# A decoder step on one core: the sample tile of the token-major projection on four column tiles, the late convolution taps over seven tiles, and the convolution's state stored in the next stage

## The reference

```python
def mix_inputs(x, pos, ln1, w_in):
    p = rmsnorm(x, ln1) @ w_in
    conv_in = p[..., :CONV_CH] * jax.nn.sigmoid(p[..., CONV_CH:2 * CONV_CH])
    # the other 1304 columns: q (512), three K/V pairs (768), gates (24)
    q = apply_rope(q, pos); keys of the three K/V pairs rotated too
    gates = jax.nn.sigmoid(p[..., o:o + COL_GATE])

def conv_module(a_ext, dw_w, dw_b, ln_g, ln_b):
    y = depthwise_conv(a_ext, dw_w, width 31) + dw_b
    return silu(layernorm(y, ln_g, ln_b))
...
p_conv.append(a[:, t_p - (CONV_W - 1):])      # out8: last 30 GLU rows of the prompt
s_conv.append(a_ext[:, a.shape[1]:])          # out9: the convolution's state of the 8 samples
```

## Time and profile before

| | |
|---|---|
| median of 3 runs | 1791.72 us (1790.69 to 1794.85) |
| time of the profiled execution | 1789.7 us |
| its span, first to last instruction | 1788.1 us |
| busy, share of the span | PE 80%, PEld 47%, DVE 37%, ACT 21%, POOL 11% |
| first stage | 0 to 339.2 us |
| second stage | 339.2 to 463.6 us |
| token-major projection of tile 8 | 305.2 to 322.8 us |

### The profile page before, as it was taken

One profiled execution on the slowest core, in us unless ns is written; L12 is line 12 of the kernel. 1 busy time (PEld: TensorE's weight loads), 2 busy tenths in 40 slices (PEclk: granted clock), 3 DMA queues, 4 the chain that ended last, 5 costly groups with the idle time before them and its releaser, 6 DMA issues. The chain is left out here.

```text
span 1788.1 us, 22662 instructions
## 1 busy us (share of the span) xinstructions
PE 1432.3 (80%) x7436; PEld 833.6 (47%) x7436; DVE 666.8 (37%) x1324; ACT 371.9 (21%) x794; POOL 192.7 (11%) x348
## 2 busy tenths in 40 slices
PE   6999899467679888852489971799999999999960
PEld 4665444267545555532245531344544454444430
DVE  2596676601258666636312237010110011011007
ACT  4000100220236555441111110111111111111113
POOL 0000011262100000003100000011111111111111
PEclk9999999779659999986689985799999999999985
DMA  6500000374331000024521100999999999999927
GB/s 240 223 1 6 12 21 21 143 218 140 89 99 32 1 1 1 1 65 123 169 101 59 63 17 31 385 412 415 398 411 411 401 409 410 409 390 409 408 104 289
DMA packets 82876, 336.98 MB, mean 188 GB/s; under 512 B 9818, under 2 KB 45787, under 8 KB 64818
## 3 DMA queue, kind: packets, MB, share of 16 engines
q1 hardware_dynamic: 64986, 287.76, 41.4%
q0 software_dynamic: 15440, 47.30, 7.7%
q10 hardware_dynamic: 2384, 1.06, 0.2%
HBM read 311.20 MB, written 29.45 MB: 191 GB/s over the span
## 5 line engine op out<-in xcount | busy, mean ns | idle before, releaser
L1695 PE MATMUL ps<-arena 128*128 128x512 f32 x544 | 241.1, 600 | 0.0
L1695 PEld LDWEIGHTS ps<-arena 128*128 128x128 f32 x544 | 102.5, 191 | 137.7 <-issue 137.6
L346 PE MATMUL ps<-arena 128*128 128x512 f32 (+3 forms) x432 | 158.9, 527 | 0.0
L499 DVE SCALAR_TENSOR_TENSOR arena<-arena 128x1024 f32<-128x1024 f32 x120 | 147.7, 1283 | 1.3
L1396 PE MATMUL ps<-arena 128*128 128x512 f32 (+1 forms) x288 | 129.6, 603 | 15.3 <-DVE arena L1491 15.3
L1749 PE MATMUL ps<-arena 128*128 128x512 f32 x272 | 120.1, 593 | 6.3 <-DMA arena<-scratch_h,ints 6.3
L1703 PE MATMUL ps<-arena 128*64 128x256 f32 x1088 | 121.2, 380 | 0.0
L301 PE MATMUL ps<-arena 128*128 128x352 f32 x384 | 116.2, 464 | 4.2 <-issue 3.7
L1000 ACT ACTIVATE arena<-ps,arena 128x640 f32<-128x640 f32 (+7 forms) x128 | 90.0, 703 | 118.6 <-DVE arena L1075 104.7
L346 PEld LDWEIGHTS ps<-arena 128*128 128x128 f32 (+1 forms) x432 | 77.2, 180 | 79.3 <-issue 72.0
L913 PE MATMUL ps<-arena 128*128 128x128 f32 x528 | 82.2, 286 | 35.8 <-ACT arena L1010 32.1
(11 more groups left out here) (357 smaller groups left out, 1588.1 us busy)
## 6 DMA issues: line engine op xcount, KB each, us to landing
arena<-in_w_gate SPq DMA_DIRECT2D x34, 2048.0 KB, 11.3
arena<-in_w_up SPq DMA_DIRECT2D x34, 2048.0 KB, 15.9
arena<-in_w_down SPq DMA_DIRECT2D x34, 2048.0 KB, 16.1
arena<-in_x_prompt SPq DMA_DIRECT2D x16, 512.0 KB, 6.7
arena<-in_cache_cmp POOLq DMA_DIRECT2D x64, 128.0 KB, 3.3
arena<-in_cache_cmp SPq DMA_DIRECT2D x64, 128.0 KB, 2.9
arena<-in_cache_sel SPq DMA_DIRECT2D x64, 128.0 KB, 2.2
arena<-scratch_y SPq DMA_DIRECT2D x16, 512.0 KB, 5.9
```

The costliest lines, as they stand in the source:

```text
L346: mm = pe.matmul(ps[:n, b + o // 512, 0:w], xT[:, k, t * P:t * P + n], w_tm[:, k, o:o + w], start=(k == 0), stop=(k == KT_ - 1))
L499: ins = dve.scalar_tensor_tensor(o, i, dw[:, c, j:j + 1], o, ALU.mult, ALU.add)
L1695: mm = pe.matmul(ps[:, bank, :], xgT_l[:, k, :], w[LARGE][:, k, :], start=(k == 0), stop=(k == KT_ - 1))
```

## The change

It has three parts. **Tile 8 of the projection** no longer runs in three pieces over the full array. Its 1304 columns are cut into four of 326 (`QTR`), and each `k` step issues four matmuls, one on each column tile of the array (32 columns wide, at 0, 32, 64 and 96), with the same stationary tokens and a quarter of the columns each. The four results lie in one PSUM bank, on the four groups of 32 partitions, and ACT brings them together by four copies (326, 326, 326 and 302 columns) and the sigmoid. **The late taps** are shared over seven tiles: `share` is 9, so tiles 0 to 5 have nine, tile 6 has eight, and tiles 7 and 8 none. **The convolution's state** is copied by ACT into `state_p` and `state_s`, in that part of `A4` which `w_cmp1` does not reach; this place lies over `a_p`, so ACT waits until all taps have been done. The five DMAs are issued by POOL in the second stage, between its loads of round 1 and the additions; POOL waits for them at that stage's end.

```diff
+        state_p, state_s = flat(A4 + 3536, CH), flat(A4 + 3536 + CH, CH)
+        QTR = COLS_TM // 4
@@ PE, projection of tile t
-                    for o, w in ((0, 512), (512, 512), (1024, COLS_TM - 1024)):
+                    if t < NQ:
+                        for o, w in ((0, 512), (512, 512), (1024, COLS_TM - 1024)):
+                            for k in range(KT_):
+                                mm = pe.matmul(ps[:n, b + o // 512, 0:w], xT[:, k, t * P:t * P + n],
+                                               w_tm[:, k, o:o + w], start=(k == 0), stop=(k == KT_ - 1))
+                    else:
                         for k in range(KT_):
-                            mm = pe.matmul(ps[:n, b + o // 512, 0:w], xT[:, k, t * P:t * P + n],
-                                           w_tm[:, k, o:o + w], start=(k == 0), stop=(k == KT_ - 1))
+                            for q in range(4):
+                                mm = pe.matmul(ps[n * q:n * q + n, b, 0:QTR], xT[:, k, t * P:t * P + n],
+                                               w_tm[:, k, QTR * q:QTR * q + QTR], start=(k == 0),
+                                               stop=(k == KT_ - 1), tile_position=(0, n * q))
@@ ACT, copies of tile t
+                    else:
+                        for q in range(4):
+                            m = min(QTR, 1280 - QTR * q)
+                            act.activation(p_sb[:n, t % 2, QTR * q:QTR * q + m], ps[n * q:n * q + n, b, 0:m], ACT.Copy)
+                        logit = ps[3 * n:4 * n, b, QTR - 24:QTR]
+                    act.activation(gates[:n, t, :], logit, ACT.Sigmoid).then_inc(sem("tm_copied"), 1)
@@ ACT, end of the first stage
-                act.wait_ge(sem("qk_turned"), TILES)
-                act.activation(xin[:TAPS - 1, 0, 0:512], ps[:TAPS - 1, 0, :], ACT.Copy)
-                act.activation(xin[:NB * NS, 1, 0:512], ps[:NB * NS, 1, :], ACT.Copy)\
+                act.wait_ge(sem("tapped"), 4 * TAPS)
+                act.wait_ge(sem("sample_tapped"), 4)
+                act.activation(state_p[:TAPS - 1], ps[:TAPS - 1, 0, :], ACT.Copy)
+                act.activation(state_s[:NB * NS], ps[:NB * NS, 1, :], ACT.Copy)\
                    .then_inc(sem("state_ready"), 1)
+                act.wait_ge(sem("state_ready"), 1)
@@ DVE
+                    dve.sem_inc(sem("sample_tapped"), 1)
-                share = -(-len(late_taps) // TILES)
+                share = -(-len(late_taps) // (NQ - 1))
@@ POOL, end of the first stage
-                pool.wait_ge(sem("state_ready"), 1)
-                pool.dma_start(out["out8"], xin[:TAPS - 1, 0, 0:512]).then_inc(sem("conv_out"), 16)
-                for s in range(NS):
-                    pool.dma_start(out["out9"][:, TAPS - 1 - NS + s, :], xin[NB * s:NB * (s + 1), 1, 0:512])\
-                        .then_inc(sem("conv_out"), 16)
-                pool.wait_ge(sem("conv_out"), 16 * (1 + NS))
@@ POOL, second stage
                 cmp_pages(pool, 1, 1)
+                pool.dma_start(out["out8"], state_p[:TAPS - 1]).then_inc(sem("conv_out"), 16)
+                for s in range(NS):
+                    pool.dma_start(out["out9"][:, TAPS - 1 - NS + s, :], state_s[NB * s:NB * (s + 1)])\
+                        .then_inc(sem("conv_out"), 16)
                 pool.wait_ge(sem("conv_gain_in"), 48)
...
                 cmp_pages(pool, 3, 1)
+                pool.wait_ge(sem("conv_out"), 16 * (1 + NS))
```

More of the change, by code:

```diff
@@ L429, in _ @@
                         act.wait_ge(sem("v_copied"), t - 1)
[L430 to L434, removed]
+                    if t < NQ:
+                        act.activation(p_sb[:n, t % 2, 0:512], ps[:n, b, :], ACT.Copy)
+                        act.activation(p_sb[:n, t % 2, 512:1024], ps[:n, b + 1, :], ACT.Copy)
+                        act.activation(p_sb[:n, t % 2, 1024:1280], ps[:n, b + 2, 0:256], ACT.Copy)
+                        logit = ps[:n, b + 2, 256:280]
+                    else:
[4 more added lines that the diff above has]
+                    act.activation(gates[:n, t, :], logit, ACT.Sigmoid).then_inc(sem("tm_copied"), 1)
                     if t >= 1:
```

## The result

The changed kernel takes 1774.12 us (median of 4 runs, 1769.28 to 1776.31) against 1792.62 us of the kernel before (4 runs, 1790.69 to 1794.85). The ratio is 0.9893, 95% interval 0.9867 to 0.9918: 1.1% faster, between 14.7 and 23.8 us. The forecast was 1773.2 us, 18.5 us less than before; the medians differ by 18.5 us.

A forecast was written before the change was run, and what follows sets the result against it. It took PE's tile 8, then POOL's stores at the first stage's end and POOL's second-stage list, as the path. Gains 12.9 + 6.6 - 1.0 = 18.5 us gave 1771.2, plus 2.0 to the median: 1773.2 us, range 1768 to 1780.

The forecast's parts named there:

- Tile 8: Projection's tile 8 on four column tiles at L1228's rate: 4.7 us instead of 17.63, a gain of 12.9 us.
- Rival 1: Tile 8 runs at the low clock's rate, 7.1 us, gaining 2.4 us less: 1775.6 us; chance 0.07.
- Rivals 3 and 4: Tile 8: column tiles take turns, 1786.1 us (chance 0.03); or also no weight load hidden, 1792.8 us (0.02).
- ACT's copies: After tile 8, four copies and a sigmoid replace three and a sigmoid: no change taken.
- The bound of 0.6: ACT's copies after tile 8: one more instruction makes them at most 0.6 us late.
- Late taps: DVE, two more taps a tile: 2.4 us more, 2.6 us of cover left, cost nothing.
- The stage's end: First stage's end: second stage starts at 332.6 instead of 339.2, before tile 8's gain, worth 6.6 us.
- One sign of being wrong: First stage's end still 4 us behind the last issue of a DMA that now comes later than 315.5.
- Five DMAs on POOL: Second stage: 2.9 us of issuing, 1.9 absorbed by a wait, round 3 1.0 us late.
- The low end, 0: Second stage's five DMAs cost 0 us if their issuing falls beside something.
- Rival 2: Second stage: POOL passes all 2.9 us on to PE's round 3: 1775.1 us; chance 0.08.
- rival 3: Tile 8: column tiles take turns, no gain there, 5.6 us in all: 1786.1 us; chance 0.03.

The follow-up runs named there:

- one-column-tile run: Changed kernel with all four quarters of tile 8's columns on one column tile and four PSUM banks: tile 8 17.69 us, distance to second stage 27.3 us.
- The split: Changed kernel with convolution state turned early, tile 8's rows stored by SP, and DVE making two of four copies: 1771.68 us, ratio 0.989.
- tiles alone: Kernel before with only tile 8 on four column tiles; seven late taps a tile and first-stage state stores stay: ratio 0.9974, distance 25.59 us.
- early state: Changed kernel with the convolution's state turned and copied before tile 8's turn: distance from tile 8's start to the second stage 14.55 us.
- state alone: Kernel before with only the state copied aside and its stores moved to the second stage: ratio 0.9996, distance 31.70 us.

## Why the prediction was right, and where it was not

The time and the direction came out as forecast, and the mechanism in its two large terms, tile 8 and the stage's end; two small terms had a step wrong. Term by term, from the distances:

- **Tile 8.** Predicted 4.7 us (its rate gives 4.76) and a gain of 12.9; measured 4.52 and 13.11. L1228's rate was a good stand-in. Rival 1 was wrong: scaled by its clock, L1186 has 0.221 ns a column, and tile 8 at a clock of 1.00 has 0.217. Rivals 3 and 4 fall with tile 8's 4.52 us; the one-column-tile run's 17.69 us shows what taking turns looks like, loads hidden. The Trainium skill's 2.38 times for three column tiles (TensorE: Matmul & The Clock Gate, section "Measured speedup vs the span model"), carried to four as an estimate, would have given 5.6 us; the trace does not agree, these matmuls reach 3.9 times. For the drain at a change of tiling mode (the Trainium skill, TensorEngine Tiling (Array Packing), section "Key Properties") the trace shows no gap: the turn starts at 310.82, before tile 8's modelled end at 310.89.
- **ACT's copies.** Predicted no change; from the turn's start to the rotation's start it is 2.00 us against 1.54 (324.38 - 322.84), 0.46 more. The step that failed is "the steps follow each other; I take no change". Four copies instead of three would have cost little: read from four banks on partitions 0 to 31 they make it 1.60 us (325.68 - 324.08), 0.06 more than before. What costs is, as far as the rows show, that each copy reads another group of 32 partitions than the one before and does not overlap with it, about 0.1 us at each of three steps. The bound of 0.6 held it. The split confirms that it is path.
- **Late taps.** Predicted nothing, 2.6 us of cover left; measured 2.48 to 2.58. That the taps of tile 7 would hold tile 8, predicted as 4.6 us, is what tiles alone shows: 4.2 us, since ACT's copies are later than predicted too.
- **The stage's end.** Predicted 6.6 us; measured 10.88 us from the end of tile 8's row stores' issue to the next stage before, and 4.09 after: 6.8. The prediction named ACT and POOL as a tie; early state shows that it was POOL. "The extra is the landing of the DMAs" is less than half of it: the stores are on record as landed 1.7 us after their issue, and by SP they cost 2.1 us or less. For the state's DMAs moved without the taps it had 3.2 us; state alone measured 2.3, since ACT's two copies then come behind the last tap. One sign of being wrong was met by its letter: the stage still starts 4 us behind a DMA issued later than 315.5 (316.77, or 315.7 with tile 8's later start taken off). These are the row stores themselves, which the prediction's numbers put at 328.33 - 12.9 = 315.4; they came 0.3 us later, as ACT's copies took longer, and no other store stands behind them.
- **Five DMAs on POOL.** Predicted 1.0 us more in the second stage; measured 0.1, less than executions differ. The step that failed is "for round 2 from 386.9 on, while L780 still runs": I took the start of the reads for the sequencer's own pace, but they waited for PE's round 0. Had I looked for what released them, the slack would have been seen. The low end, 0, was in the range. Rival 2 falls. The reads, and not these 0.1 us, are what shows it.

The sum of the measured terms is 13.1 - 0.5 + 6.8 - 0.1 = 19.3 us against 18.5. The errors are 0.2 at tile 8, -0.5 at the copies, 0.2 at the stage's end and 0.9 at the DMAs; they cancel only in part. The measured median difference of 18.5 us, anywhere from 14.7 to 23.8 by its interval and 15.3 us when measured again, can't tell the two sums apart. So the exact agreement of the times is luck; the terms' agreement within 1 us is not. A slip in the chances: rival 3, 5.6 us faster, is called faster in words, but its 0.03 is counted as the same.

What stays open: why tile 8 starts up to 1.4 us apart from execution to execution, why the stages behind the change vary by several us, why the medians give less than the distances, and what makes up the 4.1 us behind POOL's stores.

## What to carry to other kernels

Price a change at a stage's end by the whole list of things that could end it, in order of time: the taps' move was worth 0 alone and 8.7 us beside the others, since each part only uncovers the next. When an instruction is added to a queue, look for each wait behind it in that queue and what released it; slack there absorbs the addition until it is used up, and only what is left moves on to the next wait. A narrow stationary operand (32 columns) is worth spreading over four column tiles where PE is the path, but price the PSUM copies behind it by where they read and not only by their columns.

## What the runs showed of the hardware that was not expected

- Stores issued by POOL (the three of tile 8's rows, or these and then the five of the state) put the next stage 4.08 to 4.19 us behind the end of their issue, though they are on record as landed 1.7 us (the rows) or 1.8 to 2.3 us (the state) after it; the same three stores of rows issued by SP at most 1.8 us (split copies: 314.88 to 316.68).
- ACT's copies of 32x326 from PSUM followed each other with an overlap of 0.1 us where they read the same partitions (1.39 us for four), and with none where each read the next group of 32 (1.75 us).
- POOL's sequencer read page numbers ahead while nine additions of 1.2 us waited on its engine, but DMAs held it: with fifteen and twenty of them, at 0.51 us each, the reads began 0.3 to 0.4 us before the last one's end.
- Four column tiles of 32 work at 3.9 times the rate of one (4.52 and 17.69 us for the same 64 records), closer to four than L1228's 3.7 here.
- Outside the change, the same code varied between executions: the fourth stage from 97.4 to 102.8 us, and from the sixth stage's first instruction to the end from 722.2 to 731.4 us. A change of 1 us is seen in a distance inside the trace, and not in the time.
